# Layer attention by head with keys in high and low parts: a two-block transformer kernel on one core

## The chip, the cores and the metric

The kernel runs on one core of one Trainium2 chip, in one launch. The metric is the device time of a run in microseconds.

## The reference, cut to what matters

Two transformer blocks on 512 tokens of width 1024, all in float32. The first block has 16 meta tokens ahead (528 rows) and two layers, and in each layer two kinds of attention on the same normed input. The change touches only these:

```python
# diff attention: 4 heads, each with two maps (q, k of 64), values of 128
s = einsum('bhmqd,bhmkd->bhmqk', qb, k) * 64 ** -0.5      # q, k with partial rope
s = where(chunk_ids[None, :] <= cq[:, None], s, -inf)
p = softmax(s);  a = p[:, :, 0] - lam * p[:, :, 1];  do = einsum('bhqk,bhkd->bhqd', a, v)
do = rmsnorm(do, subln_gain) * (1 - lam_init) * silu(dg)
# fox attention: 8 heads of 64
s = einsum('bhqd,bhkd->bhqk', qb, k) * 64 ** -0.5 + cq[..., None] - cum_logf[:, :, None, :]
s = where(positions[None, :] <= pq[:, None], s, -inf)
fo = einsum('bhqk,bhkd->bhqd', softmax(s), v) * silu(fg)
h = h + concatenate([do, fo], axis=-1) @ w_out[l]
```

The second block (two SwiGLU networks, sparse and stick-breaking attention, memory attention) stays as it is. Its windowed attention appears below only for its timeline.

## The kernel before, in words

Each engine (PE, ACT, DVE, POOL, and SP for the DMAs) runs a hand-written list of instructions, with semaphores between the lists. Activations lie with features on partitions and tokens along the free axis. A large product is three fp32r matmuls: high part of the weights by high part of the input, high by low, low by high (`mm3`, L469). A weight chunk is loaded by SP into `raw` (`load_weights`, L421), ACT writes its fp32r high part `wh` (`split_hi`, L436), POOL subtracts for the low part `wl` (`split_lo`, L448). There are two buffers of each, and the split of chunk p waits for the tile of chunk p - 2.

**Projections** (`proj_*`, L722 to L950). Tiles of 128 features in the order dq0, fq0, dq1, fq1, ... dk0, fk0, ... (`FEATS`), then values, then eight gates. DVE scales each tile out of PSUM. For dq and dk it then rotates (`rope_dve`, L647): a product with the cosine, one with the sine on rows that SP swaps by DMA (`swap_rows`, L635), an addition. Queries go to `QA` (diff) and `QB` (fox), 8 tiles of [128, 528] in float32, one for each map or head: the 64 rows of the head are filled, the other 64 are zero, which POOL clears before each layer (L2988, L2989, L943). A key tile in `KA` or `KB` holds two maps or heads; the zeros pick one.

**Attention** (`layer_plan` L1496, class `Plan`, `attention_pe` L1069, `attention_act` L1105, `attention_dve` L1134, `attention_pool` L1213). A unit is one head (or one map) for one tile of 128 queries: n = 144, 272, 400 or 528 keys for query tiles i = 0 to 3. There are 32 diff and 32 fox units a layer, taken two by two in turn, outer loop over the query tile, inner over the heads. The score of a unit is a float32 matmul of `QA` or `QB` with `KA` or `KB` over at most 400 keys and one over the rest, with one fp32r product for the decay (fox) and one for the mask:

```python
terms.append((Q[:, m, c0:c0 + 128], K[:, m // 2, a:b], a, b, True, not fox and not masked))
```

In step s, PE transposes the probabilities of unit s - 3 (L1082), begins the scores of up to three units ahead (`begin_pe`, L1059; one ahead for n = 528, which takes two PSUM banks; two in the first 34 units of layer 0, where a bank serves the meta queries), and multiplies by the values (L1097) what step s - 1 transposed. DVE finds the maximum of unit s + 1 (L1143), ACT the exponential of unit s (L1122) and most copies of transposed probabilities; DVE mixes the two maps of a diff head (L1167 to L1173). The 16 meta keys go apart: POOL collects them for four heads (`meta_keys_pool`, L1202), which share one transpose and one product with a block-diagonal value tile (`meta_values_pool`, L1177). After the last head of a query tile comes its end (`end_pe`, `end_act`, `end_dve`): normalize, transpose, gate, high part (L1312) and low part (L1411) into `X[l]`. The last values (`vb0`) are projected under the first units (`last_values_pe`, L768; `last_values_dve` in step 2, in layer 0 step 1).

**Output projection** (`wout_pe`, L1565). Its eight tiles need all heads of the token columns they work on. The first one is made in three column pieces, the last of which waits for query tile 3; the rest are whole (`feature_tile`, L493). ACT and POOL split the first two chunks of `w_out` in attention steps 46 to 52.

## Time and profile before

| | us |
|---|---|
| median of 3 runs | 1861.98 (1860.59 to 1871.54) |
| the profiled execution | 1859.73 |
| its span, first to last instruction | 1857.9 |
| PE busy | 1829.4 (98%) |
| DVE, ACT, POOL busy | 1151.1, 769.7, 465.7 |
| mean granted TensorE clock | 1.00 of full speed |

All durations come from the one profiled execution. A matmul's record includes its way through the array and overlaps with the next, so what an instruction costs is read from the starts of neighbours, and busy PE is no proof of PE at its peak. A float32 matmul has two records. "x3" is a run of three alike. What stands in brackets is the idle time ahead and what ended it.

### The profile page before, as it was taken

To read this page: it belongs to the slowest core of one execution; us is meant where nothing else is said; L and a number is where in the kernel's file an instruction comes from. 1 tells how busy PE (TensorE), PEld (TensorE's weight loads), DVE (VectorE), ACT (ScalarE), POOL (GpSimd) and SP (SyncE) were. 2 spreads that over 40 slices of the span, in tenths; PEclk is the share of its full clock that TensorE was granted. 3 is DMA by queue.
4 is the path that set the end of the run, shared out by engine and by line. 5 is a ranking of instruction groups with operands and counts; after the bars stand their busy time and mean duration, and the time that the engine had idled before them with its cause. 6 is when DMAs were issued, how large, how long until landed. Compare 5 with 4: busy or idle time off the path is not lost.

```text
span 1857.9 us, 29611 instructions
## 1 busy us (share of the span) xinstructions
PE 1829.4 (98%) x12020; PEld 1631.3 (88%) x12020; DVE 1151.1 (62%) x1677; ACT 769.7 (41%) x1392; POOL 465.7 (25%) x322
## 2 busy tenths in 40 slices
PE   9999999999999999999999999999999999999999
PEld 8999888979988887999988877989767879999887
DVE  7542465555416657899984555646556579999531
ACT  4122455321235644444433324446565544444331
POOL 5433211354341123000034423320003420000343
PEclk9999999999999999999999999999999999999999
DMA  4222100223220012332323233200003213323232
GB/s 166 97 84 89 38 4 21 78 87 98 81 97 7 24 35 93 120 126 94 103 75 102 91 112 123 82 24 1 1 1 114 91 59 122 126 92 103 72 98 102
DMA packets 41048, 145.49 MB, mean 78 GB/s; under 512 B 5072, under 2 KB 5328, under 8 KB 40784
## 3 DMA queue, kind: packets, MB, share of 16 engines
q1 hardware_dynamic: 40912, 143.59, 22.9%
q8 instruction: 96, 1.57, 0.3%
q14 instruction: 40, 0.33, 0.1%
HBM read 140.40 MB, written 2.10 MB: 77 GB/s over the span
## 4 chain that ended last, share of the span: by engine, by line
PE 91%; DVE 5%; ACT 2%; issue 1%; DMA 1%; POOL 0%; SPq 0%; DVEq 0%; ACTq 0%
PE ps L470 23%; PE ps L471 23%; PE ps L472 23%; PE ps L1066 6%; PE ps L1097 5%; PE ps L1082 2%; PE ps L2668 1%; PE ps L2651 1%; DVE xl L560 1%; PE ps L2409 1%; PE ps L2639 1%; PE ps L1276 1%; DVE nm L1143 0%; PE ps L2654 0%; DVE scratch L613 0%
## 5 line engine op out<-in xcount | busy, mean ns | idle before, releaser
L454 POOL TENSOR_TENSOR wl<-raw,wh 128x1024 fp32r<-128x1024 f32 (+1 forms) x170 | 411.1, 2418 | 1021.8 <-ACT wh L446 1021.7
L446 ACT ACTIVATE wh<-raw 128x1024 fp32r<-128x1024 f32 (+1 forms) x178 | 188.9, 1061 | 607.1 <-PE ps L472 541.9
L470 PE MATMUL ps<-xh,wh 128*128 128x264 f32 (+3 forms) x1144 | 384.3, 336 | 6.2 <-ACT wh L446 2.5
L471 PE MATMUL ps<-xl,wh 128*128 128x264 f32 (+3 forms) x1144 | 380.8, 333 | 0.0
L472 PE MATMUL ps<-xh,wl 128*128 128x264 f32 (+3 forms) x1144 | 380.4, 332 | 0.0
L472 PE MATMUL ps<-XSh,wl 128*128 128x256 f32 (+1 forms) x864 | 283.4, 328 | 0.0
L470 PE MATMUL ps<-XSh,wh 128*128 128x256 f32 (+1 forms) x864 | 283.1, 328 | 0.3 <-DVE wl L1749 0.3
L471 PE MATMUL ps<-XSl,wh 128*128 128x256 f32 (+1 forms) x864 | 283.1, 328 | 0.0
L470 PEld LDWEIGHTS ps<-xh,wh 128*128 128x128 f32 x1144 | 215.2, 188 | 33.8 <-issue 7.8
L471 PEld LDWEIGHTS ps<-xl,wh 128*128 128x128 f32 x1144 | 215.3, 188 | 22.5 <-issue 1.0
L472 PEld LDWEIGHTS ps<-xh,wl 128*128 128x128 f32 x1144 | 215.4, 188 | 22.0
L470 PEld LDWEIGHTS ps<-XSh,wh 128*128 128x128 f32 x864 | 162.5, 188 | 16.9 <-issue 0.5
L471 PEld LDWEIGHTS ps<-XSl,wh 128*128 128x128 f32 x864 | 162.9, 189 | 16.1
L472 PEld LDWEIGHTS ps<-XSh,wl 128*128 128x128 f32 x864 | 162.2, 188 | 15.7
L470 PE MATMUL ps<-XSh,whx 128*128 128x256 f32 x496 | 139.8, 282 | 0.3 <-DVE tmpn L1986 0.2
L472 PE MATMUL ps<-XSh,wlx 128*128 128x256 f32 x496 | 139.7, 282 | 0.0
L471 PE MATMUL ps<-XSl,whx 128*128 128x256 f32 x496 | 139.3, 281 | 0.0
L1143 DVE TENSOR_REDUCE nm<-ps 128x1 f32<-128x144 f32 (+7 forms) x208 | 100.0, 490 | 55.6 <-PE ps L1066 55.2
L470 PE MATMUL ps<-wh,xh 128*128 128x256 f32 (+1 forms) x352 | 100.6, 286 | 0.3 <-DVE xb L2142 0.3
L471 PE MATMUL ps<-wl,xh 128*128 128x256 f32 (+1 forms) x352 | 99.3, 282 | 0.0
L472 PE MATMUL ps<-wh,xl 128*128 128x256 f32 (+1 forms) x352 | 99.3, 282 | 0.0
L470 PEld LDWEIGHTS ps<-XSh,whx 128*128 128x128 f32 x496 | 93.3, 188 | 0.7 <-DVE tmpn L1986 0.4
(419 smaller groups left out, 3472.6 us busy)
## 6 DMA issues: line engine op xcount, KB each, us to landing
raw<-wstream SPq DMA_DIRECT2D x176, 512.0 KB, 3.3
rawx<-wpairs SPq DMA_DIRECT2D x44, 512.0 KB, 3.5
raw<-wpairs SPq DMA_DIRECT2D x24, 512.0 KB, 3.5
raw<-wstream SPq DMA_DIRECT2D x10, 528.0 KB, 3.3
h<-xT SPq DMA_DIRECT2D x4, 528.0 KB, 5.8
out<-h SPq DMA_DIRECT2D x8, 256.0 KB, 4.2
xs<-wpairs SPq DMA_DIRECT2D x2, 512.0 KB, 4.5
HF<-wpairs SPq DMA_DIRECT2D x2, 512.0 KB, 5.4
```

The lines of the kernel that those rows point to most:

```text
L446: e.activation(wh[p % 2][:, 0:n], raw[c % 2][:, 0:n], ACT.Copy).then_inc(*w_hi(p))
L454: e.tensor_tensor(wl[p % 2][:, 0:n], raw[c % 2][:, 0:n], wh[p % 2][:, 0:n].bitcast(F32), ALU.subtract).then_inc(*w_lo(p))
L470: e.matmul(o, w_h, x_h, start=start, stop=False)
L471: e.matmul(o, w_h, x_l, start=False, stop=False)
L472: return e.matmul(o, w_l, x_h, start=False, stop=stop)
L560: e.scalar_tensor_tensor(dl, src, gain, dh.bitcast(F32), ALU.mult, ALU.subtract).then_inc(*v_lo(st, k))
L1066: r = e.matmul(ps[:, x.o0 + lo:x.o0 + hi], lhsT, rhs, start=start, stop=stop)
L1082: r = e.transpose(ps[0:b - a, 128 * j:128 * j + 128], plan.source(u)[:, a:b], ident)
L1097: r = e.matmul(PS[:, lo + x.cols[0]:lo + x.cols[1]], buf[0:b - a, 128 * j:128 * j + 128], x.value(j, b - a), start=j == 0 and (x.first or ...
L1143: e.tensor_reduce(nm[:, u % 8:u % 8 + 1], PS[:, lo:lo + x.n], AX.X, ALU.max, negate=True).then_inc(*peak(name, u))
L1276: r = e.transpose(ps[:, 128 * j:128 * j + nq], src[:, 128 * j:128 * j + 128], ident[0:nq, 0:nq])
L2409: r = e.matmul(PS[:, 512 * HELD + 512 * mt:512 * HELD + 512 * mt + 64], ww[:, a0:a0 + 128], Y[s][:, v, v:v + 64, j], start=v == 0 and j == ...
```

## The change

- `QA` and `QB` become fp32r tiles: the 64 rows of the head hold the high part of the query and the other 64 rows the low part. DVE writes the scaled or rotated query to scratch, ACT casts it (two instructions of 64 partitions), DVE subtracts (two more). No clears. The 16 meta queries of layer 0 are kept in float32 in `QZ`.
- The keys of one head or map are copied by SP to both partition halves of a slot of `xs` (two DMAs, two slots); ACT casts the high part, DVE subtracts the low one. Two heads are done in the value stage, 14 in attention steps given by a list. The parts lie in a new tile `KX`, in the free weight buffers `wh` and `wl`, or in query tiles that are done.
- The score is two fp32r products with the same queries.
- Units run by head: a diff head c with its four query tiles and two maps, a fox head with its four query tiles. PSUM output columns, sums, quads of meta keys and ends follow: an end now covers one diff head (gate in one instruction) or two fox heads, for all 512 tokens. The block-diagonal meta values are rewritten by POOL for each quad.
- In layer 0 the bank for the meta queries is set aside in units 0 to 10 and 17 to 24 only.
- The output projection makes the rows of heads 0 to 2 for tiles 0 and 1, then the rows of head 3 (k = 3 and 7) for both.

```diff
+            if kind == "dq" and c:
+                on.wait_ge(*v_lo["dq", l, c - 1])
...
-                on.wait_ge(*p_one["clear", l, 0])
-                for j in range(2):
-                    e.tensor_tensor(QA[64 * j:64 * j + 64, 2 * c + j, c0:c0 + n], u[64 * j:64 * j + 64],
-                                    v[64 * j:64 * j + 64], ALU.add).then_inc(*roped(*key, "add", j))
+                e.tensor_tensor(u, u, v, ALU.add).then_inc(*roped(*key, "add", 1))
...
+        def query_high_act(e, on, key):
+            src, to = query_parts(key)
+            on.wait_ge(*(roped[key + ("add", 1)] if key[0] == "dq" else v_out[key]))
+            for j, b in enumerate((0, 64)):
+                r = e.activation(to[b:b + 64, j, :], src[b:b + 64], ACT.Copy)
+            r.then_inc(*a_out(*key, "high"))
...
+            for j, b in enumerate((0, 64)):
+                r = e.tensor_tensor(to[64 - b:128 - b, j, :], src[b:b + 64], to[b:b + 64, j, :].bitcast(F32), ALU.subtract)
+            r.then_inc(*v_lo(*key))
+
+        KEYS = [("diff", 0, 0), ("diff", 0, 1), ("fox", 0, 0), ("fox", 0, 1), ("diff", 1, 0), ("diff", 1, 1), ("fox", 1, 0),
+                ("diff", 2, 0), ("diff", 2, 1), ("fox", 1, 1), ("fox", 2, 0), ("diff", 3, 0), ("diff", 3, 1), ("fox", 2, 1),
+                ("fox", 3, 0), ("fox", 3, 1)]
+        KEY_STEP = dict(zip(KEYS[2:], (0, 3, 5, 7, 11, 14, 16, 19, 28, 31, 33, 36, 44, 47)))
...
+            return [last_score(l, *was[kind, c], q)] if (kind, c) in was else [tile["vb0", l, 1]]
...
+            on.wait_ge(*(roped["dk", l, 2 + i, "sin"] if i < 2 else v_lo[("key", l) + KEYS[i - 2]]))
+            for b in (0, 64):
+                e.dma_start(xs[b:b + 64, n % 2, :], src).then_inc(d_key[n % 4], 16)
...
+            e.activation(high, xs[:, KEYS.index((kind, c, q)) % 2, :], ACT.Copy).then_inc(*a_out("key", l, kind, c, q))
...
+            e.tensor_tensor(low, xs[:, KEYS.index((kind, c, q)) % 2, :], high.bitcast(F32), ALU.subtract).then_inc(
+                *v_lo("key", l, kind, c, q))
...
+                if kind == "fq":
+                    query_high_act(e, on, key)
+                    query_high_act(e, on, ("dq", l, c))
...
-                for q, Q in enumerate(Q_of[l]):
-                    e.memset(Q[:, :, :], 0.0).then_inc(*p_one("clear", l, q))
...
+                if x.lows:
+                    on.wait_ge(*v_lo[x.lows])
...
+                if plan.layer is not None:
+                    for head in KEY_STEP:
+                        if KEY_STEP[head] == s - 1:
+                            key_low_dve(e, on, plan.layer, *head)
...
+            for i in range(4):
+                a = quad.cols[0] + w * i
+                r = e.tensor_copy(VMeta[quad.kind][32 * i:32 * i + 16, a:a + w], V[0:16, 0, w * n:w * n + w])
...
-                    terms.append((Q[:, m, c0:c0 + 128], K[:, m // 2, a:b], a, b, True, not fox and not masked))
+                    terms.append((Q[:, m, c0:c0 + 128], khigh[:, a:b], a, b, True, False))
+                    terms.append((Q[:, m, c0:c0 + 128], klow[:, a:b], a, b, False, not fox and not masked))
...
+            for c in range(2):
+                claim(on, pair(("wout", l, c)), halves, v_out["wout", l, c])
+                product(c, (0, 1, 2, 4, 5, 6), True)
+                if c == 0:
                     end_pe(e, on, plans[l], *plans[l].held)
+            for c in range(2):
+                product(c, (3, 7), False).then_inc(*tile("wout", l, c))
...
+            for stop, heads in ((CHUNK["va1", l, 0], KEYS[0:2]), (CHUNK["gate", l, 4], KEYS[2:4]),
+                                (CHUNK["wout", l, 2], KEYS[4:])):
+                load_weights(e, on, first, stop)
+                first = max(first, stop)
+                for head in heads:
+                    key_copies(e, on, l, *head)
```

ACT makes a key's high part at the end of the step listed, DVE its low part at the end of the next.

## Rows read from the trace of the kernel before

**Rows 1.** chain of waits, whole span, shares by engine.

```profile
PE 91%; DVE 5%; ACT 2%; issue 1%; DMA 1%; POOL 0%; SPq 0%; DVEq 0%; ACTq 0%
```

**Rows 2.** windows by stage: busy (instructions) of PE, PEld, DVE, ACT, POOL; clock; DMA.

```profile
211.15:321.20 110.05, 106.61 (x792) 89.78 (x790) 72.22 (x202) 63.34 (x195) 13.42 (x50) 1.00 0.03 11
321.20:330.07 8.87, 8.87 (x78) 8.84 (x77) 3.89 (x9) 1.26 (x2) 0.00 (x0) 1.00 0.01 2
330.07:335.90 5.83, 5.83 (x50) 5.83 (x50) 3.08 (x2) 2.22 (x3) 2.39 (x1) 1.00 0.14 40
565.70:667.10 101.40, 99.62 (x680) 84.72 (x679) 66.02 (x177) 61.18 (x186) 13.35 (x50) 1.00 0.04 12
667.10:675.60 8.50, 8.50 (x77) 8.45 (x77) 3.92 (x9) 1.27 (x2) 0.00 (x0) 1.00 0.01 2
675.60:681.20 5.60, 5.60 (x27) 4.58 (x27) 3.08 (x2) 2.81 (x4) 2.41 (x1) 1.00 0.11 25
```

**Rows 3.** PE timeline (start, us), layer attention, map units of 400 and 528 keys.

```profile
264.22 0.49 PE L1082 MATMUL ps<-identR,scratch 128*128 128x128 f32 x3
...
265.25 0.91 PE L1097 MATMUL ps<-VA,PT 128*128 128x128 f32 x6
...
302.36 0.61 PE L1082 MATMUL ps<-identR,scratch 128*128 128x128 f32 x4
302.81 1.06 PE L1066 MATMUL ps<-KA,QA 128*128 128x400 f32 x4
...
303.73 0.44 PE L1082 MATMUL ps<-identR,Pb 128*128 128x128 f32 x2
```

**Rows 4.** PE timeline, second block: fp32r keys in two products, 384 and 512 keys.

```profile
1264.40 0.52 PE L1082 MATMUL ps<-identR,Pb 128*128 128x128 f32 x3
...
1265.17 0.60 PE L1097 MATMUL ps<-VSW,PT 128*128 128x64 f32 x4
...
1300.10 0.60 PE L1082 MATMUL ps<-identR,Pb 128*128 128x128 f32 x4
1300.46 0.72 PE L1066 MATMUL ps<-KSW,QN 128*128 128x512 f32 x2
...
1301.08 1.05 PE L1097 MATMUL ps<-VSW,PT 128*128 128x64 f32 x8
```

**Rows 5.** timeline of ACT and POOL, weight split after the first output tile.

```profile
330.33 1.06 ACT L446 ACTIVATE wh<-raw 128x1024 fp32r<-128x1024 f32 x1 [4.01 <-PE ps L472]
...
331.47 2.39 POOL L454 TENSOR_TENSOR wl<-raw,wh 128x1024 fp32r<-128x1024 f32 x1 [15.68 <-ACT wh L446]
```

**Rows 6.** PE and POOL timelines around the clears of the query tiles.

```profile
25.90 0.36 PE L470 MATMUL ps<-xh,wh 128*128 128x264 f32 x1 [1.25 <-ACT wh L446]
...
378.40 3.63 POOL L943 MEMSET QB<- 128x4224 f32 x1
...
384.53 0.47 PE L470 MATMUL ps<-xh,wh 128*128 128x512 f32 x1 [1.21 <-ACT wh L446]
```

**Rows 7.** DVE and PE timelines, begin of the second layer's attention.

```profile
560.23 0.42 DVE L674 COPY tmpn<-ps 16x256 f32<-16x256 f32 x1 [0.62 <-PE ps L700]
...
565.93 0.48 DVE L788 TENSOR_SCALAR VB<-ps,small 128x256 f32<-128x256 f32 x1 [2.37 <-PE ps L472]
...
567.51 0.30 PE L1082 MATMUL ps<-identR,Pb 128*128 128x128 f32 x1
```

**Rows 8.** groups by line, 212 to 321 us, one 512-column high and low part.

```profile
L1411 DVE TENSOR_TENSOR xl<-xb,xh 128x512 fp32r<-128x512 f32 x6 | 4.1, 680 | 0.0
...
L1312 ACT ACTIVATE xh<-xb 128x512 fp32r<-128x512 f32 x6 | 3.8, 629 | 1.8 <-DVE xb L1358 1.7
```

**Rows 9.** DMA issues of the page, and the issue of one row swap.

```profile
raw<-wstream SPq DMA_DIRECT2D x176, 512.0 KB, 3.3
...
L645 SPq DMA_DIRECT2D xs<-xb x64: 624/628/762, 24.8 to 463.4; - x64
```

**Rows 10.** one line's durations, ns min/median/max: the cosine product.

```profile
L656 DVE TENSOR_TENSOR scratch<-xb,cst x16: 697/1704/2726, 26.1 to 467.1; 128x528 f32<-128x528 f32 x12, 128x512 f32<-128x512 f32 x4
```

More of the change, by code:

```diff
@@ L834, in proj_dve @@
             st = "n%d" % l
-            QB = Q_of[l][1]
             on.wait_ge(*a_one[st, "scale"])
@@ L1111, in attention_act @@
                     split_hi(e, on, PART["wout", plan.layer, s // 4 - 11])
-                if s == 32 and plan.layer == 0:
-                    on.wait_ge(*one_mm["meta", "fox", 0, "pv"])
                 if s < len(units):
@@ L1173, in attention_dve @@
                     e.scalar_tensor_tensor(p0, p1, q, p0, ALU.mult, ALU.add).then_inc(*mixed(name, u))
+                if plan.layer is not None:
+                    for head in KEY_STEP:
+                        if KEY_STEP[head] == s - 1:
+                            key_low_dve(e, on, plan.layer, *head)
                 for key, k in plan.ends.get(s, []):
```

272 lines of the change are left out of this document (179 added, 93 removed).

## The prediction

> **What bounds the kernel now.** I read the page first: in the chain of waits PE holds 91% of the span [rows 1], so the time is PE's own work, and a change pays where it takes work off PE or ends one of its few stalls. Next the windows by stage [rows 2]. The attention of layer 0 lasts 110.05 us and keeps PE busy for 106.61; that of layer 1 lasts 101.40 with 99.62 busy. The granted clock is 1.00 in all of these stages, that is the 2.4 GHz level. DVE is busy for 72.22 and 66.02 us of them and ACT for 63.34 and 61.18, so both have a third or more to spare. Then the PE timeline, for what one score costs: from the start of the transposes ahead of it to the start of the matmuls behind it. Last the idle gaps, two of which the change touches [rows 6].
>
> The profiled execution took 1859.73 us, of them 1857.9 in the span; the median of the three runs is 1861.98. I sum against 1859.73 and add the 2.25 between them at the end.
>
> **Scores (removed work).** A map unit is one query tile against its keys. Now: four transposes and a 528-key score take 303.73 - 302.36 = 1.37 us; three and a 400-key score take 265.25 - 264.22 = 1.03 [rows 3]. The second block already does what the change introduces: fp32r queries and keys in two products, with the same transposes ahead. There three transposes and 384 keys take 0.77 us, four and 512 keys 0.98 [rows 4]. For 400 keys I add 2 x 16 columns at 2.4 GHz: 0.78, a saving of 0.25. 528 keys stay split into 400 and 128: 0.98 less 2 x 112 columns (0.09) plus two short products at 0.11 each (8.50 us over 77 instructions in the layer-1 row of the first output tile [rows 2]) is 1.11, a saving of 0.26. For 272 keys I take half, 0.12. At 144 keys an instruction costs its 0.11 whatever it streams: nothing. That is 0.63 per head, and the fox heads, whose extra product for the decay stays, save the same. With 16 heads it is 10.1 us a layer. The other end: all 1344 columns of a head give back two passes at 2.4 GHz, 1.12 us, 17.9 a layer, but that forgets the floor of 0.11. I take 11 a layer, near the rows: **-22**, between -20.2 and -35.8.
>
> **Output projection.** Its first tile now comes in three column pieces of 128 to 264 columns and takes 8.87 us in layer 0, against 5.83 for the next one, and 8.50 against 5.60 in layer 1 [rows 2]. Afterwards it takes whole rows; the four transposes inside it stay (0.4). So 8.87 - 5.83 - 0.4 and 8.50 - 5.60 - 0.4: **-5.1**. But tiles 0 and 1 now both hold their weights until the rows of head 3 come. Weights of tile 2 need tile 0 done: now the split ends at 331.47 + 2.39 = 333.86, 3.79 us after tile 0's end at 330.07 [rows 2, 5], hidden under tile 1. Afterwards only a quarter of tile 1 (1.46 and 1.40) lies there: a new stall of 2.33 and 2.39, **+4.7**. The rows of head 3 themselves are not late: after the transposes PE has three quarters of tile 1 (4.4 and 4.2) to hide gate, high and low part (some 0.65 each, as the parts in [rows 8]). The end is bounded by 0 (another order of the splits hides it) and +7.6.
>
> **Clears removed.** POOL clears both query tiles before each layer, 3.63 us apiece, ahead of a weight split; PE then waits 1.25 us at 25.90 and 1.21 us at 384.53. The page names ACT's high part, but that is old by then; POOL's low part behind the clears came last [rows 6]. Without them the low part is there before PE asks: **-2.5** (at least 0, at most this).
>
> **Beginning of attention.** The first fox key has its high and low part where the last values' weights lie, so ACT makes it at step 0 only after that tile, at about T = 565.7 in layer 1. DVE makes the low part at the end of step 1, T + 1.6 (0.63 and 0.68 [rows 8] behind one semaphore each). Its last values stand at step 2 in layer 1: today they begin at 560.23, long before T, with one of them left at 565.93 [rows 7]; afterwards all five instructions (three of about 0.4, two of 0.48: 2.1 us) and the next maximum queue behind the key. The first mixed map then comes at about T + 4.7; today PE takes it at 567.51, T + 1.8 [rows 7]. PE has 1.6 us of scores to do meanwhile in both. +3.0 in layer 1. In layer 0 the values stand at step 1 ahead of the key, and only the key's 0.68 and its wait come in: +1.3. Together **+4.3** (0 to +7).
>
> **Key parts during attention.** 14 of the 16 heads of a layer have theirs made inside the loop: ACT +14 x 0.63 = 8.8 us, DVE +14 x 0.68 = 9.5 [rows 8], less about 1.8 for gating in one instruction where there were four. DVE then has 74 to 80 us of work in 90 to 99, 82%, where it had 65%. PE's idle time in the loops is 3.4 and 1.8 us now [rows 2]; with both helpers in order and so much fuller I let it grow by 2.5 a layer: **+5** (0 to +17, all of it that the scores give but the uncovered start). Behind a waiting ACT stand its exponentials, and behind these DVE's mixing and PE's transposes.
>
> **Key copies.** SP copies each head's keys to both halves of one of two slots. The chain of a slot is two issues at 0.63, landing, high part, low part. Landing is not in the trace for this size: below, nothing beyond the issue; above, 3.3 us, the landing of a 512 KB load [rows 9]; the copy is 270 KB from SBUF to SBUF. I take 3.3, the nearest row. The chain is 1.26 + 3.3 + 0.63 + 0.68 = 5.9 us. In the list of steps six links a layer have only three to four steps between the low part that frees the slot and the next high part; a step is about 90 / 64 = 1.4 us, less at the start, where the keys are few. The two early ones are late by 1 to 2 us, the others by little, and PE has work queued for half of that: **+3** (0 to +6). The weight loads queued behind the copies on SP are not wanted before the splits of steps 46 and 50.
>
> The Trainium skill (SBUF — State Buffer, "Can I just issue two DMAs to hit both halves?") says that two copies on the two partition halves serialize, at a mere 6% over one. No run here shows that. It speaks against this way of doubling the keys, and is what would feed the third rival below.
>
> **Projections.** Per head pair ACT gets four casts of 64 partitions (2.5 us) and DVE two subtractions instead of one product, four in all (2.7, at the 0.68 of [rows 8]), in 11.7 us of PE tiles. The weight split stands behind the casts on ACT and would start 0.4 us later, with about 2 us of room before PE needs the low part. DVE's cosine product takes 0.70 us alone and 2.73 while POOL subtracts weights [rows 10]. The new subtractions can meet the same. I put **+0.5** (0 to +16).
>
> The Trainium skill (SBUF — State Buffer, "Who interferes with whom") has this as an exclusive lock between a DVE instruction with two SBUF inputs and a GpSimd one that reads SBUF; by that rule the trace's 2.73 is a wait for POOL's end. The fourth rival is this rule carried through.
>
> The memory of the per-head meta values costs POOL some 48 short copies a layer instead of 12; it is busy for 13.4 us of 100 [rows 2]: nothing.
>
> **Sum.** -22 - 5.1 + 4.7 - 2.5 + 4.3 + 5 + 3 + 0.5 = -12.1. 1859.73 - 12.1 = 1847.6 for a profiled execution, and 1850 for the median.
>
> **Rivals.** A measurement of this kernel tells about 1% from no change: below 1843.4 or above 1880.6 us.
>
> First, full cover: PE's queue is deep enough that neither the fuller DVE nor the copies reach it, and half of the late start is caught up. For it: today's idle of 3.4 and 1.8 us at 65% DVE. Against: the loop's maximum sits in a chain with the exponential, and wide scores are begun one step ahead only. -12.1 - 5 - 3 - 2 = -22, 1840.
>
> Second, the loop goes at the pace of DVE and ACT: PE gets faster and waits for what it gained. For it: 82% is an average, and the ends of heads and the key parts fall together. Against: 18% stay free. The 22 is lost, of which 5 are counted: 1850 + 17 = 1867.
>
> Third, slower than before: the key copies land later than 3.3 us. Place: the six close links a layer; ACT stands in front of its exponentials. Each microsecond more of landing costs up to 12 over both layers. Slower than before from 1.0 us more (12.1 / 12), slower by over 1% from 2.6 more. At 2 us more: 1850 + 24 = 1874. Against: the far larger load lands in 3.3.
>
> Fourth, DVE meets POOL in the projections and ACT's casts, then the split behind them, come late by 2 us in each of eight pairs: +16, 1866. Against: the room of 2 us.
>
> That the two products don't cost less than the old one is excluded by [rows 4].
>
> **Chances.** Forecast 43%, full cover 27%, pace of DVE and ACT 14%, late copies 10%, projections 6%. The terms' bounds about the likeliest give 1840 to 1858; full cover reaches down to 1832 if half of the scores' open part comes too, and the others up to 1868: that is the range. Faster by over 1%: 32% (full cover but for a little, and the lower edge of the forecast). Slower by over 1%: 6% (half of the late copies, some of the rest). Within: 62%.
>
> **What would show it.** Right: score groups at line 1066's successor some 0.25 us shorter at 400 and 528 keys; attention of some 104 us in layer 0 and 97 in layer 1; PE idle for 2.3 us before output tile 2 in both layers; no gap at tile 3 of layer 0's and tile 2 of layer 1's projections; DVE's last values of layer 1 after the tile. Wrong: ACT idle for a DMA before the key casts by more than 3 us a layer, PE idle over 10 us in an attention, gaps in the projections, or a score that costs as before.

## The result and the profile after the change

The changed kernel takes 1887.28 us, the median of four runs, against 1861.39 for the kernel before beside it: ratio 1.0133, 95% interval 1.0118 to 1.0148, slower by over 1%. The prediction said 1850 us, faster than before, with 1832 to 1868 as its range. The profiled execution took 1879.27 us, 1877.2 of them in the span, 19.3 more than the span before. Several terms of the sum came out; the loss comes from places to which it gave little or nothing.

The chain of waits on the page of the profile, shares by engine, as in [rows 1]: PE fell from 91% to 85% and DVE rose from 5% to 8%, a first sign that a faster TensorE now waits for others.

```profile
PE 85%; DVE 8%; ACT 3%; issue 2%; POOL 1%; DMA 1%; SPq 0%; ACTq 0%; DVEq 0%; POOLq 0%
```

Windows of the changed kernel, columns as in [rows 2]: the attention of layer 0, output tiles 0 and 1, the stretch behind them, and the same for layer 1. An attention is counted here from the end of the last value product to the start of the first output product.

```profile
210.13:328.87 118.74, 103.29 (x791) 92.23 (x790) 80.31 (x207) 71.07 (x213) 30.18 (x98) 0.94 0.15 37
328.87:341.20 12.33, 12.33 (x102) 12.21 (x100) 4.20 (x7) 2.49 (x4) 0.09 (x1) 1.00 0.01 1
341.32:349.50 8.18, 5.89 (x37) 5.92 (x37) 4.96 (x4) 3.09 (x5) 4.96 (x2) 0.79 0.38 128
573.65:684.03 110.38, 95.19 (x680) 85.66 (x680) 75.97 (x187) 69.19 (x206) 30.12 (x98) 0.97 0.16 40
684.03:695.90 11.87, 11.87 (x54) 9.39 (x52) 4.18 (x7) 2.44 (x4) 0.03 (x1) 1.00 0.00 0
696.03:704.90 8.87, 6.54 (x23) 5.18 (x22) 5.56 (x5) 4.30 (x7) 4.66 (x2) 0.81 0.35 118
```

PE is busy for less, 103.29 and 95.19 us against 106.61 and 99.62 [rows 2], yet each attention is some 9 us longer: PE stands for 15.4 and 15.2 us where it stood for 3.4 and 1.8. Over 10 us in an attention was one of the prediction's own signs of being wrong. And the granted clock, the third number from the end, is no longer 1.00. Windows of 4 us of PE alone show where it fell (length, PE busy, clock, DMA share, GB/s):

```profile
212.00:216.00 4.00, 2.71 (x20) 0.84 0.29 68
216.00:220.00 4.00, 4.00 (x18) 0.50 0.46 107
220.00:224.00 4.00, 2.91 (x18) 0.80 0.15 34
300.00:304.00 4.00, 2.96 (x12) 0.51 0.00 0
304.00:308.00 4.00, 4.00 (x23) 0.64 0.38 131
344.00:348.00 4.00, 4.00 (x22) 0.57 0.53 162
576.00:580.00 4.00, 3.54 (x16) 0.57 0.29 68
```

0.50 is the lower level, 1.2 GHz. With four more windows of layer 1 (0.81 and 0.76 at 656 and 660 us, 0.93 and 0.64 at 696 and 700 us behind the output's stall) this comes to 27.4 us at the lower level. At half speed at most half of that is lost, 13.7 us. Each fall comes during or behind a wait of PE, these five and one of 1.82 us at 657.09 (in brackets: idle time, and what ended it):

```profile
213.69 0.52 PE L1166 MATMUL ps<-wl,QB 128*128 128x272 f32 x2 [1.29 <-ACT Pb L1220]
...
301.04 1.04 PE L1166 MATMUL ps<-QA 128*128 128x400 f32 x2 [1.82 <-ACT Pb L1220]
...
343.61 0.36 PE L474 MATMUL ps<-xh,wh 128*128 128x264 f32 x1 [2.29 <-POOL wl L458]
...
576.46 0.75 PE L1166 MATMUL ps<-KX,QA 128*128 128x272 f32 x2 [2.80 <-DVE VB L882]
...
698.36 0.48 PE L474 MATMUL ps<-xh,wh 128*128 128x512 f32 x1 [2.33 <-POOL wl L458]
```

The product of a wait that names the exponential (line 1220) is the first of a score: it waits for its PSUM bank, which the exponential of an earlier map unit gives back. Layer 1's attention has 11 such waits, 7.8 us in all. The reverse does not hold: behind waits of 1.41 and 1.46 us at 224 and 256 us the clock stayed at 1.00.

### The profile page after: what moved, and what is told of

It reads as the page before. It is cut to its first block, busy times and chain, and to the rows that moved or that the text cites. A ratio compares the mean times of both kernels' runs of the same rounds, so it can differ in the third digit from the quotient of the medians.

```text
span 1877.2 us, 29806 instructions
## 1 busy us (share of the span) xinstructions
PE 1820.4 (97%) x11948; PEld 1631.1 (87%) x11948; DVE 1202.2 (64%) x1717; ACT 804.3 (43%) x1456; POOL 484.3 (26%) x391
## 4 chain that ended last, share of the span: by engine, by line
PE 85%; DVE 8%; ACT 3%; issue 2%; POOL 1%; DMA 1%; SPq 0%; ACTq 0%; DVEq 0%; POOLq 0%
PE ps L474 23%; PE ps L475 23%; PE ps L476 23%; PE ps L1197 4%; PE ps L1166 4%; PE ps L1182 2%; DVE nm L1245 2%; PE ps L2811 1%; POOL wl L458 1%; PE ps L2794 1%; DMA raw<-wstream 1%; DVE xl L564 1%; PE ps L1393 1%; PE ps L2782 1%; PE ps L2552 1%
## 5 line engine op out<-in xcount | busy, mean ns | idle before, releaser
L458 POOL TENSOR_TENSOR wl<-raw,wh 128x1024 fp32r<-128x1024 f32 (+1 forms) x170 | 416.0, 2448 | 1026.5 <-ACT wh L450 1026.5
L474 PE MATMUL ps<-xh,wh 128*128 128x264 f32 (+1 forms) x1120 | 380.2, 339 | 8.9 <-POOL wl L458 6.9
L475 PE MATMUL ps<-xl,wh 128*128 128x264 f32 (+1 forms) x1120 | 376.7, 336 | 0.0
L476 PE MATMUL ps<-xh,wl 128*128 128x264 f32 (+1 forms) x1120 | 376.2, 336 | 0.0
L1245 DVE TENSOR_REDUCE nm<-ps 128x1 f32<-128x144 f32 (+5 forms) x208 | 101.1, 490 | 59.6 <-PE ps L1166 58.9
L1220 ACT ACTIVATE Pb<-ps,nm 128x528 f32<-128x528 f32 (+7 forms) x144 | 79.4, 552 | 36.3 <-DVE nm L1245 35.6
```

The costliest lines, as they stand in the source:

```text
L458: e.tensor_tensor(wl[p % 2][:, 0:n], raw[c % 2][:, 0:n], wh[p % 2][:, 0:n].bitcast(F32), ALU.subtract).then_inc(*w_lo(p))
L474: e.matmul(o, w_h, x_h, start=start, stop=False)
L475: e.matmul(o, w_h, x_l, start=False, stop=False)
L476: return e.matmul(o, w_l, x_h, start=False, stop=stop)
L1220: e.activation(plan.slot(s)[:, 0:x.n], PS[:, lo:lo + x.n], ACT.Exp, bias=nm[:, s % 8:s % 8 + 1], accum_out=x.total[0]).then_inc(*prob(name ...
L1245: e.tensor_reduce(nm[:, u % 8:u % 8 + 1], PS[:, lo:lo + x.n], AX.X, ALU.max, negate=True).then_inc(*peak(name, u))
```

## The experiments

Times are medians; "L0" and "L1" are the two attentions of the profiled execution, counted as above. The kernel before has 109.92 and 101.26 by this rule, the changed kernel 118.74 and 110.38. The profiled execution of the changed kernel is its fastest of four, 8 us below the median, so a difference of medians and one of profiles can disagree by that much; where they do, both are given.

**The two factors apart.** Four kernels: scores by one f32 product or by two fp32r ones, with and without the 14 key parts per layer inside the loop.

```diff
-                    terms.append((Q[:, m, c0:c0 + 128], khigh[:, a:b], a, b, True, False))
-                    terms.append((Q[:, m, c0:c0 + 128], klow[:, a:b], a, b, False, not fox and not masked))
+                    terms.append((Q[:, m, c0:c0 + 128].bitcast(F32), khigh[:, a:b].bitcast(F32), a, b, True,
+                                  not fox and not masked))
```

> The changed kernel with each score made by one f32 product (query block by the high key part) in place of the two fp32r products; the low key parts are still made, and left out of the score. It leaves the order by head and all work of ScalarE and VectorE as they are. Numbers against the changed kernel, whose median is 1887.3 us and whose two attentions idle TensorE for 15.4 and 15.2 us. Theory L (the idle time is the latency of the loop from score to maximum to exponential to the claim of a PSUM bank, in an order that gives the wide units of each head one step of lead): TensorE gets some 11 us busier in each layer, and part of the idle time goes under it, since a longer score covers part of the same waits: 7 to 8 us of idle left in each attention, the time up by 8 to 14 us in all. Rival P (TensorE's own work sets the pace and its waits stand beside it): idle time stays at 15 us in each attention, the time is up by 20 to 24 us.

1891.19 us (1.0174, 1.0153 to 1.0196), 4 more by the medians and 9.6 by the profiled executions (1888.84 against 1879.27), with 11.2 and 9.2 us of idle time left. That is nearer to theory L (7 to 8 us) than to rival P (15), but less went under the longer scores than it put down. The second edit takes the key parts out:

```diff
-                khigh, klow = key_home(l, kind, c, q)
+                khigh, klow = key_home(l, "diff", 0, q)
...
-        KEY_STEP = dict(zip(KEYS[2:], (0, 3, 5, 7, 11, 14, 16, 19, 28, 31, 33, 36, 44, 47)))
+        KEY_STEP = {}
```

> The changed kernel without the 14 key parts that each attention makes between its steps: all heads use the parts of the first differential head, and the 28 copies on the queue, 28 conversions on ScalarE and 28 subtractions on VectorE of the two layers are left out, so the scores of the other heads are those of wrong keys. Against the changed kernel (1887.3 us). Theory W (the load of the key parts on ScalarE and VectorE, some 0.7 us each in front of an exponential or a maximum, idles TensorE): 14 x 0.7 us per layer come back in large part, the time falls by 15 to 27 us, the idle time in each attention to 5 us or less. Theory L (lead of the wide units): the bank claims behind wide units stay, 9 to 12 us of idle are left in each attention, the time falls by 5 to 12 us, most of it the wait at the beginning of layer 1 (2.80 us and the clock behind it), where ScalarE's conversion of the first forgetting key waits for the last value tile.

1869.83 us (1.0050, 1.0029 to 1.0070), 17 less, as theory W said; but 12.4 and 9.2 us of idle time stay, as theory L said. Neither holds it all. Both edits together leave the order by head and what comes with it (the ends by head, and POOL's rewriting of the meta values, which takes POOL from 13.4 to 26 us busy in each attention):

> The order by head alone: the changed kernel with one f32 product per score (query block by a high key part) and without the 14 key parts per layer (all heads use those of the first differential head), which leaves TensorE, ScalarE and VectorE the work of the kernel before, in the new order, with the new output projection. Its scores are those of wrong keys. Against the kernel BEFORE (1860.4 us; idle 3.4 and 1.8 us in the attentions). Theory L (the order by head costs time by itself, since each head's wide units have one step of lead): 3 to 6 us more of idle in each attention, and with the stall before output tile 2 and its clock some 1866 to 1874 us. Rival (the order is free, all the idle time comes with the key parts and the shorter scores): attentions within 1.5 us of those before, 1860 to 1863 us.

1877.81 us, ratio to the kernel before 1.0092 (1.0077 to 1.0107), more than even theory L put down. The windows of the attentions, first of the order alone, then with fp32r products, then with key parts and f32 products:

```profile
210.11:330.62 120.51, 110.51 (x792) 89.90 (x790) 72.08 (x193) 63.50 (x197) 25.93 (x98) 1.00 0.03 10
575.66:684.34 108.68, 104.33 (x679) 84.98 (x679) 65.61 (x169) 60.52 (x186) 26.31 (x98) 1.00 0.04 11
```

```profile
210.24:324.93 114.69, 102.32 (x792) 91.76 (x790) 71.96 (x193) 63.67 (x197) 26.07 (x98) 0.96 0.03 10
568.13:669.13 101.00, 91.83 (x680) 82.33 (x679) 65.69 (x169) 60.48 (x186) 26.42 (x98) 1.00 0.04 12
```

```profile
209.84:333.38 123.54, 112.29 (x790) 90.75 (x790) 80.18 (x207) 71.43 (x213) 29.63 (x98) 0.99 0.15 36
576.82:693.48 116.66, 107.45 (x680) 87.19 (x680) 75.73 (x187) 69.28 (x206) 29.90 (x98) 0.97 0.16 38
```

The first pair is the find of the study. DVE and ACT do the work of before (72.08 and 65.61 against 72.22 and 66.02 [rows 2]), the clock is 1.00, PE issues as many matmuls, and the attentions are longer by 10.6 and 7.4 us: **the order alone costs 18.0 us**. About half of it shows as idle time (10.0 and 4.4 against 3.4 and 1.8), the rest, 8.9 us, as more busy time for the same instructions. The matmuls themselves are hardly longer: their durations add up to 246.7 us against 245.4 in L0 and 223.8 against 222.4 in L1. So most of the rest is records that overlap less.

From there the fp32r products take off 5.8 and 7.7 us. Where a fall of the clock lies in an execution, half of its time at the lower level is lost at most: 5.1 us in L0 of the second kernel, 1.7 and 3.4 in the third, 6.9 and 3.4 in the changed kernel. With that taken out the two attentions add up to 211.2 before, 229.2 in the new order, 210.6 with fp32r products, 235.1 with key parts, and 218.8 with both. So with all of that bound taken out the products give 16 to 19 us and the key parts cost 6 to 8. With nothing taken out the same four kernels give 11 to 14 for the products and 11 to 13 for the key parts; what they are at one clock lies between, and the 18.0 of the order does not depend on it.

**Why the order costs.** In both kernels a 528-key score has its claim one step ahead of its exponential, any other two or three. Before, the 16 wide units of a layer stand at the end of it; by head, every 16 units have three wide ones in a row and one alone. By the lists of both kernels 17 steps of a layer have only one score begun ahead, in either order; but before they form two stretches, and by head eight, and behind nearly each of the eight the list, run down to one, is filled again with several claims in one step. Cutting the fourth tile to 400 keys makes no unit wide; the last key block is left out of it. In layer 0 the cut order also takes the bank for the meta queries as the kernel before does, in the first 34 units.

```diff
-                n, c0, key = M + 128 * (i + 1), M + 128 * i, (kind, l, c)
-                fox, wide = kind == "fox", i == 3
+                n, c0, key = M + 128 * min(i + 1, 3), M + 128 * i, (kind, l, c)
+                fox, wide = kind == "fox", False
```

> The order by head alone (as in the run of that order), with the fourth query tile's scores cut from 528 to 400 keys in both layers, so that no unit is wide and none has a lead of one step; leads and banks as in the kernel before (2 steps and 3 banks for the first 34 units of layer 0, else 3 and 4). The last key block is left out of the fourth tile's scores and values. It is compared with the kernel before, cut in the same way. Theory L (the lead of one step of the wide units, spread over the four heads, is what the order costs): the two cut kernels' attentions are within 2 us of each other in each layer, where the uncut ones differ by 10.6 and 7.4 us. Rival (the order costs by something else: the ends and output banks, the switching of keys): 5 us or more remain in each.

> The kernel BEFORE with the fourth query tile's scores cut from 528 to 400 keys in both layers; the last key block is left out of its scores and values. The reference for the cut order by head: 32 score products of 128 columns, 32 masks or gate products and 24 value products of the last block fewer in the two layers each, some 10 us less work of TensorE in each attention; the attentions some 100 and 92 us if nothing else changes, the idle time no more than the 3.4 and 1.8 us of the uncut kernel under theory L and its rival alike.

1847.12 and 1840.87 us, so 6.3 apart where the uncut kernels are 17.2 apart. The cut order by head, then the cut kernel before:

```profile
210.43:313.51 103.08, 98.33 (x714) 81.06 (x714) 68.45 (x193) 60.73 (x197) 25.69 (x98) 1.00 0.03 11
557.02:651.30 94.28, 91.23 (x605) 76.02 (x603) 62.06 (x169) 57.80 (x186) 26.34 (x98) 1.00 0.04 12
```

```profile
211.48:311.82 100.34, 97.81 (x715) 81.08 (x714) 68.51 (x202) 60.64 (x195) 13.26 (x50) 1.00 0.04 12
556.50:648.20 91.70, 90.82 (x605) 76.00 (x603) 62.35 (x178) 58.45 (x186) 13.19 (x50) 1.00 0.04 13
```

2.7 and 2.6 us of the 10.6 and 7.4 remain, a little above the 2 us of theory L and well below the 5 of its rival: 12.7 of the 18.0 us go with the wide units. POOL is as busy in the cut order (25.69 and 26.34 us), so its rewriting is at most part of the rest. The cleaner case is layer 1, where only the wide units went and 2.6 us are left of 7.4; in layer 0 the bank of the meta queries moved with them. The cut took the two PSUM banks of a wide unit and its longer maximum and exponential away together with its short lead, so which of these it is stays open.

**Issuing scores later.** Units behind a wide one claim a bank in the step in which its holder's exponential runs. This edit makes them wait a step:

```diff
-                    while nxt < n and nxt <= s + units[nxt].ahead:
+                    while nxt < n and nxt <= s + units[nxt].ahead and (layer is None or units[nxt].was < max(s, 0)):
```

> The changed kernel where the scores of a unit are issued no earlier than the step after the exponential of the unit that held its PSUM bank; in the changed kernel the units behind a head's wide units claim a bank in the very step in which its holder's exponential runs, and the value products of that step stand behind the claim. Against the changed kernel (1887.3 us; idle 15.4 and 15.2 us). Theory L (these claims are the cost of the order by head): of the claims seen, 0.68 + 0.89 us at the wide units of each head and 0.4 to 1.0 elsewhere, most goes: 4 to 6 us less idle time in each attention, some clock falls with it, the time down by 8 to 15 us. Rival (the claims show a loop whose length stays the same wherever the wait stands): the wait moves to the transposes and value products, the time is within 3 us, or higher since the lead of the scores is shorter.

1880.37 us (1.0101, 1.0084 to 1.0118). L1 took 110.25 us, against 110.38: the pair of 0.68 and 0.89 at a head became one wait of 1.40. So in the attentions the rival is right: the wait stands wherever the loop is cut. The median is 6.9 us below the changed kernel's, but the profiled execution 3.2 above its (1882.43 against 1879.27), and nothing in the attentions shows a gain.

**The beginning of layer 1.** ACT and DVE timelines of the changed kernel there:

```profile
573.75 0.64 ACT L754 ACTIVATE wl<-xs 128x528 fp32r<-128x528 f32 x1 [6.55 <-PE ps L476]
...
574.43 0.71 DVE L759 TENSOR_TENSOR wl<-xs,wl 128x528 fp32r<-128x528 f32 x1 [6.90 <-ACT wl L754]
...
576.33 0.86 DVE L882 TENSOR_SCALAR VB<-ps,small 128x256 f32<-128x256 f32 x2
```

The key part waits for the last value tile (the high part is put into its weights' memory), and the value copies queue behind it, as forecast. The edit puts the copies first:

```diff
-                if plan.layer is not None and s == units[0].ahead - 1:
+                if plan.layer is not None and s == 1:
                     last_values_dve(e, on, plan.layer)
...
-        KEY_STEP = dict(zip(KEYS[2:], (0, 3, 5, 7, 11, 14, 16, 19, 28, 31, 33, 36, 44, 47)))
+        KEY_STEP = dict(zip(KEYS[2:], (1, 3, 5, 7, 11, 14, 16, 19, 28, 31, 33, 36, 44, 47)))
```

> The changed kernel with the last values of an attention's first steps copied before the key parts: both copies in step 1 (now step 3 on ScalarE, step 2 on VectorE in layer 1), and the first forgetting key's parts one step later. Theory E (the 2.80 us wait at the beginning of layer 1 is the value copies queued behind a subtraction, which waits for a conversion that waits for the end of the last value tile): the wait falls to 0.5 to 1.5 us, the clock fall at 576 us (3.4 us at the lower level) goes, the time is down by 2.5 to 4 us; layer 0, whose wait of 1.29 us stands elsewhere, keeps it. Rival: the wait is only moved to the first forgetting score, which needs those parts, nothing gained (within 1 us).

1882.11 us by the median, 5 less, and 1885.12 in the profiled execution, 6 more. The wait went over to the first forgetting score, which needs that key:

```profile
581.71 0.42 PE L1166 MATMUL ps<-wl,QB 128*128 128x144 f32 x2 [2.43 <-DVE wl L759]
```

2.43 for 2.80, and in layer 0 a new one of 1.99 us. The rival's mechanism is right: the place in memory ties the key to the tile. The times by themselves decide nothing here.

**The end of a head.** ACT timeline of the changed kernel ahead of the wait at 301 us: 

```profile
299.13 0.21 ACT L1417 ACTIVATE small<-small 128x4 f32<-128x4 f32 x1 [1.98 <-DVE small L1457]
299.37 0.20 ACT L1419 ACTIVATE small<-small 128x4 f32<-128x4 f32 x1
299.48 1.04 ACT L450 ACTIVATE wh<-raw 128x1024 fp32r<-128x1024 f32 x1
300.43 0.47 ACT L1220 ACTIVATE Pb<-ps,nm 128x272 f32<-128x272 f32 x1
```

```diff
-            elif key[0] == "diff" and k == 2:
+            elif key[0] == "diff" and k == 3:
...
                 e.activation(ms, ms, ACT.Ln, scale=1.0 / 128, bias=1e-5).then_inc(*a_end(*key, "ln"))
```

> The changed kernel with ScalarE's logarithm and exponential of a differential head's end one step later, behind that step's exponential of the scores, and the two conversions of output weights in steps 46 and 50 behind the exponential in place of ahead of it. Theory Q (ScalarE stands 1.97 us behind VectorE's small products of the head's end and then 1.04 us in the weights, with ready scores behind it; the claim of 1.82 us at 301 and 657 us is this): these waits fall to 0.7 us or less, their clock falls (6.8 and 3.4 us at the lower level) go, the time is down by 5 to 8 us. Rival: VectorE now waits for ScalarE one step later with maxima behind it, the wait only changes its engine, the time is within 2 us.

1891.04 us, 4 more. The rival is right: the wait changed its engine, and doubled:

```profile
312.87 0.59 PE L1197 MATMUL ps<-VA,PT 128*128 128x128 f32 x2 [3.62 <-DVE tmpn L1463]
```

DVE now waits for ACT, and the next head's values for the bank that DVE frees. All four edits together (the fourth follows below):

> All four together: scores issued after the holder's exponential, last values first, the end's logarithm a step later, output tile 2's weights in the last head's key memory. If the four are separate waits, the idle time in each attention falls from 15 to 5 or 6 us, the granted clock stays near 1.00, and the time falls by 25 to 32 us against the changed kernel, to 1855 to 1862 us, level with the kernel before. If ScalarE's and VectorE's load is the real bound (76 and 69 us busy of 111, in a chain with TensorE), the waits come back in other places: 1867 to 1875 us.

1878.94 us (1.0096), above even its second case; waits of 2.12 and 3.62 us for the bank that a head's end frees are among those left.

**The stall before output tile 2.**

```diff
+        def weights_home(p):
+            if PARTS[p][0] == "wout" and PARTS[p][2] == 2:
+                kx = KX[:, :, :, :].rearrange("p a b c -> p (a b c)")
+                return kx[:, 0:1024], kx[:, 1024:2048]
+            return wh[p % 2], wl[p % 2]
```

> The changed kernel with the weight parts of output tile 2 put into the memory of the last head's key parts, free once its scores are made, so that they need not wait for output tile 0. Against the changed kernel. Theory D (the stall before output tile 2 is the wait for its weights, and the clock falls behind it): 2.29 and 2.33 us of stall go, and with the clock at 1.00 another 1.7 us in each layer, 8 us in all. Rival 1: only the stall goes, 4.6 us. Rival 2: it moves to output tile 3, whose weights take the place of tile 1's, and nothing is gained (within 2 us).

1876.11 us (1.0087, 1.0072 to 1.0102), 11 less by the medians and 4.5 by the profiled executions. Neither stall is left, and no fall of the clock behind the outputs, as theory D said. L0 was longer, 122.25 us at a clock of 0.90, with falls that the changed kernel's profile does not have; the falls differ between executions of one kernel.

**The clock.** Unread products in three kinds of gap:

```diff
+            for _ in range(count):
+                e.matmul(PS[:, 512 * bank_:512 * bank_ + 112], ident, ident[:, 0:112], start=True, stop=True,
+                         skip_group_check=True)
```

> The changed kernel with products of the identity, whose result nobody reads, put into three kinds of gap of TensorE: 5 (layer 0) and 12 (layer 1) of 128x112 f32 behind the last value tile, some 0.19 us each, and 10 before output tile 2 of each layer. Nothing else moves; the gaps in the middle of the attentions (at 301 and 657 us) get none. Theory C (the granted clock falls because TensorE stood still for 1.3 to 2.8 us there): in these places the granted clock stays at 1.00, and the 6.9, 3.4, 3.4 and 3.4 us at the lower level go, which is 8.5 us of time at half speed: time down by 6 to 9 us, while the falls at 301 and 657 us stay. Rival: the clock falls for another reason (the denser fp32r products of the new scores, or the kernel's total activity), the falls stay where they are, and the time is within 2 us of the changed kernel's or above it.

1878.16 us (1.0094, 1.0079 to 1.0109), 9 less by the medians, as theory C said, but only 1 by the profiled executions. Behind the filled gaps:

```profile
576.00:580.00 4.00, 3.94 (x27) 1.00 0.22 51
...
600.00:604.00 4.00, 3.11 (x16) 0.66 0.30 68
...
700.00:704.00 4.00, 4.00 (x18) 1.00 0.68 238
```

1.00 at 576 and 700 us, where it was 0.57 and 0.64, but 0.66 at 600, behind waits of 0.68 and 0.89 us. In layer 0 the products stood ahead of the wait of 1.29 us, not in it; wait and fall stayed. The counterpart puts a gap into the kernel before:

```diff
         def last_values_dve(e, on, l):
+            if l:
+                on.wait_ge(*token_done("vb0", l, 4, 5))
+                for i in range(4):
+                    e.tensor_tensor(scratch[:, i, 0:T], KA[:, i, 0:T], KA[:, i, 0:T], ALU.add)
```

> The kernel BEFORE the change, with one wait added: at the beginning of layer 1's attention VectorE makes four sums of 128x512 that nobody reads, ahead of the copies of the last values, so that TensorE stands still there for some 3 us; nothing of the change is in it. Theory C (a stand of TensorE of 1.3 us or more is what makes the granted clock fall in the changed kernel): the granted clock, 1.00 throughout in the kernel before, falls to 0.50 for some 3.4 us behind the wait, and the time is up by the wait and another 1.7 us, 4.5 to 5 us in all. Rival (the falls come from the fp32r scores or from the density of the new attention): the clock stays at 1.00, the time is up by the wait alone, 3 us.

1865.73 us, 5.1 more than before. PE stood for 3.84 us, and the clock of a kernel that has none of the change fell:

```profile
564.00:568.00 4.00, 2.15 (x19) 1.00 0.00 0
568.00:572.00 4.00, 2.01 (x9) 0.53 0.00 0
572.00:576.00 4.00, 4.00 (x24) 0.62 0.02 6
576.00:580.00 4.00, 4.00 (x34) 1.00 0.00 0
```

So neither fp32r scores nor the new order are needed for it; a stand of PE of this length is enough. It stayed at the lower level for 6.8 us, twice as long as put down, but part of that lies in the wait itself, so the time came out as theory C had it.

**Load.** DVE's 14 low parts per layer moved to GpSimd:

```diff
-                        if KEY_STEP[head] == s - 1:
-                            key_low_dve(e, on, plan.layer, *head)
...
+                        if KEY_STEP[head] == s - 1:
+                            key_low(e, on, plan.layer, *head)
```

> The changed kernel with the subtraction of 14 of the 16 low key parts of each layer on GpSimd in place of VectorE (GpSimd is busy 30 us of each attention, VectorE 80 and 76). Against the changed kernel (1887.3 us; idle 15.4 and 15.2 us). Theory V (the key parts cost 6 us of idle time per layer, as the kernel without them showed, since VectorE's 14 subtractions of 0.7 us stand ahead of maxima and copies): 2 to 4 us of idle go in each attention, the time falls by 4 to 10 us. Rival A (ScalarE's conversions ahead of the exponentials are the costly half, or GpSimd's slower subtraction comes late to the scores that need it): idle time as before or higher, the time within 3 us or above.

1875.80 us (1.0078, 1.0050 to 1.0106), 11 less by the medians, but 1 more by the profiled executions (1880.02). L1 took 105.39 us, 5.0 less, with 12.0 idle for 15.2; 1.7 of the 5.0 can be the clock's, which had 3.4 us at the lower level there for 6.9. L0 took 124.12, at a clock of 0.86. So VectorE's subtractions are part of what the key parts cost, 3 us or more in L1, where leaving the parts out altogether gave 6 by the same count. ScalarE's conversions were not moved. The combination:

> The pieces that helped or should: low key parts on GpSimd, output tile 2's weights in the last head's key memory, the two weight conversions of ScalarE behind the exponential of their step, and unread products in the wait at the beginning of layer 1 (12) and ahead of the first claim that waits in layer 0 (6). If the three theories (VectorE's queue, the weights' stall, the clock behind a stand) are right, the attentions idle TensorE for 9 to 11 us, the clock falls at the beginnings are gone, and the time is 1862 to 1870 us. If the low parts on GpSimd come late: 1872 to 1878 us.

1869.92 us (1.0048, 1.0031 to 1.0066), at the upper end of its first case, with 13.2 and 11.6 us of idle time left instead of 9 to 11. A new wait showed the fourth key's copy late:

```profile
581.17 0.64 ACT L763 ACTIVATE wh<-xs 128x528 fp32r<-128x528 f32 x1 [2.36 <-DMA xs<-KA]
```

```diff
-        KEY_STEP = dict(zip(KEYS[2:], (0, 3, 5, 7, 11, 14, 16, 19, 28, 31, 33, 36, 44, 47)))
+        KEY_STEP = dict(zip(KEYS[2:], (0, 4, 7, 9, 12, 14, 16, 19, 28, 31, 33, 36, 44, 47)))
```

> The combined kernel of the last runs (low key parts on GpSimd, output tile 2's weights in the last head's key memory, ScalarE's weight conversions behind the exponential, unread products in two waits) with four key parts one to two steps later: steps 4, 7, 9 and 12 in place of 3, 5, 7 and 11. In the combined kernel ScalarE waited 2.36 us for the copy of the fourth of them with exponentials behind it, and TensorE 2.24 us. If late copies are the cause: both waits go, the granted clock at 580 to 592 us stays up, 3 to 6 us less than the combined kernel's 1869.9 us. Rival: the copy waits on the parts before it, all are late together, and the wait moves to the scores of the second head: within 2 us.

1868.74 us. The waits went and L1 fell from 108.67 to 105.38, at a clock of 1.00 for 0.97, but the median moved by 1.2 us only, no more than its rival allowed (2). Last, unread products in a wait of layer 0:

```diff
                 x = plan.units[u]
+                if plan.layer == 0 and u == 10:
+                    on.wait_ge(*prob[plan.name, 8])
+                    fill(e, 2, 6)
                 ps = claim(on, *x.banks, prob[plan.name, u])
```

> The kernel with the later key parts, and six more unread products ahead of the claim of the first head's third wide unit in layer 0, where TensorE stood 1.41 to 1.60 us and the clock fell in most kernels of the new order (20 us at the lower level in the combined kernel between 220 and 252 us). Theory C: the fall goes with the stand, 6 to 10 us less than without the six products, 1856 to 1862 us. Rival: the clock falls at the next of the small waits (1.04 us at 241 and 244 us) all the same: within 3 us.

1865.90 us, ratio to the kernel before 1.0014 (0.9999 to 1.0029): level with it. In L0 the window of 224 to 236 us, at 0.50 without the six products, is at 1.00 with them, and L0 fell from 120.24 to 114.85; a fall remains at 236 to 246, with waits of 1.04 and 1.05 us in it. But this profile is the fastest of ten executions (1860.82 to 1867.92). The medians differ by 2.8 us, which is the rival's case (within 3) and less than theory C had (6 to 10). No version that makes all the scores beats the kernel before.

## Why the prediction was wrong, step by step

- **Scores, -22: right in kind, too high by 3 to 6 us, or more if the clock's bound takes too much out.** PE timeline of a 400-key score, to lay beside [rows 3], in the kernel before and then in the changed one:

```profile
264.55 0.84 PE L1066 MATMUL ps<-KA,QA 128*128 128x400 f32 x2
```

```profile
246.42 0.61 PE L1166 MATMUL ps<-wh,QA 128*128 128x400 f32 x2
246.87 0.19 PE L1166 MATMUL ps<-maskR,identR 128*128 128x64 f32 x1
246.90 0.86 PE L1197 MATMUL ps<-VB,PT 128*128 128x64 f32 x6
```

  From the first product to the next work it takes 246.90 - 246.42 = 0.48 us, with no transposes in it; before it was 265.25 - 264.55 = 0.70. The saving is 0.22 where 0.25 was forecast. The kernels with and without the two products give 16 to 19 us with the clock taken out, 11 to 14 without.
- **Output projection, -5.1 and +4.7: right.** Tiles 0 and 1 take 12.33 and 11.87 us against 14.70 and 14.10 before [rows 2], 4.6 less. The stalls are 2.29 and 2.33, forecast 2.33 and 2.39. What was missed is the clock behind them: 3.4 us at the lower level each, up to 3.4 lost in all.
- **Clears, -2.5: right as far as seen.** The waits of 1.25 and 1.21 us are gone from the projections of both layers, and the first attention starts 1.2 us earlier.
- **Projections, +0.5: right.** From 40 to 60 us DVE is busy for 18.65 us where it was 13.40, and PE for 20.00 in both. The fourth rival falls, and with it the Trainium skill's lock ("SBUF — State Buffer", "Who interferes with whom") as a cost to PE here: VectorE grew fuller beside GpSimd's 9.88 us, and no product came late. The lock itself agrees with the trace: a key's low part on VectorE took 2.46 us from 123.75 on, beside GpSimd's subtraction of 2.39 us from 123.26 on, and 0.70 in the attentions.
- **Beginning of attention, +4.3: right in layer 1, luck in layer 0.** PE stands for 2.80 us in layer 1, forecast 3.0, and the kernel without the key parts has no such wait. It priced the value copies behind the key; the failed remedy shows that the key itself, tied to that tile by its memory, is as late (2.43 us). In layer 0 the forecast was 1.3 and PE stands for 0.37 and 1.29 us, but the longer wait is not the key's: it is there without key parts too, and the order alone has it with 1.02 us.

```profile
213.22 0.52 PE L1166 MATMUL ps<-KX,QB 128*128 128x272 f32 x2 [1.25 <-ACT Pb L1220]
```

- **Key copies, +3: mis-sized, towards less.** DMA issues of the page:

```profile
xs<-KA SPq DMA_DIRECT2D x32, 132.0 KB, 2.3
xs<-KB SPq DMA_DIRECT2D x32, 132.0 KB, 2.4
```

  2.3 and 2.4 us from issue to landing, where 3.3 was taken; in the attentions ACT waited for one copy, 0.7 us. The third rival, slower than before by late copies, had the right sign by the wrong mechanism. The Trainium skill's rule that copies on the two partition halves serialize ("SBUF — State Buffer", "Can I just issue two DMAs to hit both halves?") was not tried.
- **Key parts in the loop, +5: the failed step.** Their own cost was placed in the right range: with copies and beginning it was 12.3 in the sum, and the kernels without them give 6 to 8 with the clock's bound taken out, 11 to 13 without. But this term also stood for all growth of idle time, and it was worked out from how full DVE and ACT are. The order costs 18.0 us with both no fuller. The second rival, the pace of DVE and ACT, failed with it: they are 68% and 60% busy in the first attention. The text had the cause in hand, "wide scores are begun one step ahead only", and used it against full cover without asking what becomes of that lead when wide units are spread over the heads.
- **No term for the clock: the second failed step.** [Rows 2] show 1.00 in all their windows, in a kernel whose attentions have no wait over 1 us. The change brought waits of 1.3 to 2.8 us, four of them in the forecast's own list, and none was priced with a fall: up to 10.3 us in the attentions and 3.4 behind the outputs. It would have had to be priced as a chance and not as a rule. The kernel before has waits of 1.25 and 1.21 us in its projections [rows 6] with the clock at 1.00 around them. And the stall of 2.3 us before output tile 2 had a fall behind it in both layers of the changed kernel, in layer 0 alone of the order by itself, and in neither layer of the kernel without key parts.

The sum for the profiled executions: forecast -12.1, measured +19.5 (1879.27 against 1859.73), 31.6 apart. Order +18.0, clock +13.7, scores -18.6 instead of -22 (+3.4), key parts with copies and beginning 8.2 instead of 12.3 (-4.1): 31.0. Inside the attentions these parts add up by construction, since each is the difference of two of the four kernels and the clock's part is what was taken out; so the closeness says only that little happened outside. The clock's part is an upper bound, and order, products and keys are taken one after the other; the other way round the products give 16.3 and the key parts 5.9. The median lies another 6.4 us up, with mean clocks of 0.986 to 0.989 where the profiled execution has 0.993.

## What to carry to other kernels

A reordering is a change of the software pipeline: list, step by step, which items are begun and which buffer each claims, for the old order and the new, before counting cycles; a single late class of items spread through the loop can cost more than the instruction change gains. Where the profile shows the granted clock at 1.00 in a kernel without long waits, price each new wait of TensorE of about a microsecond or more with a possible fall behind it. And a wait that is moved in an in-order queue comes back on another engine unless the resource behind it (a bank, a piece of memory) is freed earlier.

## What was not expected of the hardware

- The granted clock fell at stands of TensorE of 1.29 to 3.84 us, for 3.4 or 6.8 us, in kernels of either order; in layer 0 of the kernel with the logarithm a step later it was down for most of the first 35 us, with waits of 1.29 and 1.20 us in them, and the attention had a mean of 0.86. It is not a fixed rule of one wait: the order by head with f32 products had waits of 1.41 and 1.45 us in its attentions at 1.00 throughout, and stalls of 2.3 us went without a fall, while one of 0.89 us, 2.9 us after one of 0.68, had a fall.
- The same kernel's executions differ with it. The changed kernel's four lie at a mean clock of 0.993 (1879.27 us) and 0.986 to 0.989 (1886 to 1889 us), so a single profile understates or overstates the loss. The kernel before has 1860 us at 1.000 in most of its executions, but 1870.8 to 1871.3 at 0.991 in three of those beside the experiments.
- Unread products that stand in a wait can keep the clock up behind it: L0 was 5.4 us shorter with six of them, and had 6.9 us at the lower level for 20.4. By the medians the gain was 2.8 us.
- GpSimd took 1.29 to 1.34 us (once 1.58) for a 128x528 subtraction that VectorE does in 0.70, and layer 1's attention was still 5.0 us shorter with it there.
